# Gate and up products of layer 0's FFN by one level of Strassen's scheme (seven quarter-size products for eight)

## The reference

```
D_MODEL = 1024; D_FF = 2816
def channel_mixer(x, l, P):                     # layer 0
    h = rms_norm(x, P['norm_ffn'][l])
    a = silu(einsum('btd,df->btf', h, P['ffn_w_gate'][0])) * einsum('btd,df->btf', h, P['ffn_w_up'][0])
    return einsum('btf,fd->btd', a, P['ffn_w_down'][0])
```

## Time and profile before

| What | Value |
|---|---|
| three runs, median (lowest to highest) | 1901.38 us (1901.1 to 1902.55) |
| span of the profiled execution, first to last instruction | 1898.2 us |
| TensorE matmul busy | 1845.5 us (97%) |
| VectorE busy | 519.3 us (27%) |
| ScalarE busy | 365.9 us (19%) |
| gate and up products of layer 0, first to last start | 569.4 to 725.9 us |

### The profile page before, as it was taken

The page is one execution under the profiler, slowest core; times in us unless marked ns, Lnnn a source line. Parts: engine busy times, 40 slices in busy tenths (PEclk is TensorE's granted clock), DMA queues, the critical chain, the costliest instruction groups (busy, mean ns, idle before and its releaser), DMA issues.

```text
span 1898.2 us, 28175 instructions
## 1 busy us (share of the span) xinstructions
PE 1845.5 (97%) x11949; PEld 1285.5 (68%) x11949; DVE 519.3 (27%) x1150; ACT 365.9 (19%) x754; POOL 135.2 (7%) x226
## 2 busy tenths in 40 slices
PE   8999999999999999999999999999799999999998
PEld 5889878786678888878888878777533343433434
DVE  3454441527321000043635234363310000000000
ACT  2241334332010000014214333310110000100101
POOL 3000001304100000000100020220000000000000
PEclk9999999999999999999999999999899999999999
DMA  9833699999999978698429998999739999599992
GB/s 273 278 116 115 218 309 326 348 317 373 358 372 376 319 280 309 221 330 315 141 73 305 337 356 307 336 384 333 266 121 371 366 387 405 221 341 386 374 409 112
DMA packets 254690, 563.83 MB, mean 297 GB/s; under 512 B 11949, under 2 KB 149393, under 8 KB 254288
## 3 DMA queue, kind: packets, MB, share of 16 engines
q1 hardware_dynamic: 235232, 500.14, 74.3%
q0 software_dynamic: 18544, 58.58, 9.2%
q10 hardware_dynamic: 784, 3.25, 0.5%
HBM read 547.74 MB, written 196.63 MB: 392 GB/s over the span
## 4 chain that ended last, share of the span: by engine, by line
PE 94%; DMA 2%; DVE 2%; issue 1%; ACT 1%; POOL 0%; ACTq 0%; DVEq 0%; POOLq 0%
PE PS L867 33%; PE PS L1414 15%; PE PS L794 8%; PE PS L1440 8%; PE PS L1315 4%; PE PS L1275 4%; PE PS L787 3%; PE PS L1289 3%; PE PS L911 3%; PE PS L1376 2%; PE PS L904 2%; PE PS L1462 1%; PE PS L1211 1%; PE PS L802 1%; PE PS L1185 1%
## 5 line engine op out<-in xcount | busy, mean ns | idle before, releaser
L867 PE MATMUL PS<-h,ring 128*128 128x264 f32 x2816 | 655.2, 389 | 0.0
L867 PEld LDWEIGHTS PS<-h,ring 128*128 128x128 f32 x2816 | 528.5, 191 | 106.9 <-issue 21.3
L1579 ACT COPY z<-PS 128x264 f32<-128x264 f32 (+3 forms) x307 | 130.5, 444 | 854.2 <-PE PS L867 529.2
L1414 PE MATMUL PS<-ring,z 128*32 128x512 f32 (+1 forms) x1440 | 210.5, 522 | 1.2 <-ACT z L1579 1.2
L1414 PE MATMUL PS<-arena,z 128*32 128x512 f32 (+1 forms) x1056 | 190.1, 535 | 0.0
L1414 PEld LDWEIGHTS PS<-ring,z 128*32 128x32 f32 x1440 | 68.0, 110 | 125.7 <-issue 110.1
L794 PE MATMUL PS<-h,ring 128*128 128x264 f32 x512 | 115.3, 386 | 1.6 <-DVE h L1967 1.6
L794 PEld LDWEIGHTS PS<-h,ring 128*128 128x128 f32 x512 | 97.2, 190 | 18.6 <-issue 2.0
L1440 PE MATMUL PS<-arena,z 128*32 128x512 f32 x432 | 104.0, 593 | 0.0
L1414 PEld LDWEIGHTS PS<-arena,z 128*32 128x32 f32 x1056 | 55.0, 110 | 53.5 <-issue 53.4
L1275 PE MATMUL PS<-z,ring 128*128 128x264 f32 x384 | 87.3, 388 | 0.0
(11 more groups left out here) (319 smaller groups left out, 1805.5 us busy)
## 6 DMA issues: line engine op xcount, KB each, us to landing
out_win_s<-in_cache_win_kv SPq DMA_DIRECT2D x128, 1023.5 KB, 11.1
ring<-in_w_in SPq DMA_DIRECT2D x88, 1024.0 KB, 6.7
out_win_s<-in_cache_win_kv SPq DMA_DIRECT2D x32, 1022.0 KB, 14.1
ring<-in_moe_w_gate SPq DMA_DIRECT2D x28, 1024.0 KB, 9.7
arena<-in_moe_w_up SPq DMA_DIRECT2D x22, 1024.0 KB, 11.5
ring<-in_moe_w_up SPq DMA_DIRECT2D x22, 1024.0 KB, 8.7
ring<-in_moe_w_down SPq DMA_DIRECT2D x20, 1024.0 KB, 11.0
arena<-in_moe_w_down SPq DMA_DIRECT2D x18, 1024.0 KB, 10.4
```

Of the source, the lines that this page charges most:

```text
L867: last = mm(bank(l, "p", j)[:, 0:T], w[:, k, P * (j % 2):P * (j % 2) + P], h[:, k, :], start=(k == 0), stop=(k == KT - 1))
L1414: last = mm(m_bank("c", "gu", g, b, w, r)[BLK * j:BLK * j + BLK, 0:n], hs[:, k, P * r + BLK * j:P * r + BLK * j + BLK], v3(slot_ap(set_slo ...
L1579: return nc.scalar.copy(out, in_)
```

## The change

A chunk holds 256 columns and 1024 features, so it is cut into four quarters, [4 feature tiles of 128] by [128 columns]: a11 and a12 for the first column tile, a21 and a22 for the second (first index the column tile, second the half of the features). `h` is cut too, by features and by token columns, 132 each: h11, h12, h21, h22. The products of a chunk, which were 16 matmuls of 264 columns, become seven products of 4 matmuls of 132 columns, 28 in all. The form is the one with four sums on either side: for the weights s1 = a21 + a22, a21 <- a11 - a21 (in place, called s3), s2 = a22 - s3, s4 = a12 - s2; for `h` four sums once (`hd`). The seven results stand in four half-filled bank pairs ("xa", "ya", "xb", "yb"; some products add into the same half) and VectorE adds them up.

VectorE makes all weight sums (`weight_sums`, four operations of 128x512 for a chunk), those of the first three chunks between `wo` and `xnorm`, later ones three chunks ahead of their use; the four sums of `h` (`input_sums`); and the sums of the results (`first_sums`, `second_sums`). ScalarE takes silu in two parts. The slot of a chunk is released when "yb" of that chunk is full. The names of some semaphores that nothing used are dropped as well. The core of the diff:

```diff
-                for i in range(FF // P):
-                    plan((0, "fg", i), 2 * (i % 2))
-                    plan((0, "fu", i), 2 * (i % 2) + 1)
+                for q in range(CH_FFG):
+                    for name in ("xa", "ya", "xb", "yb"):
+                        plan((0, name, q), 2 * (q % 4) + (name[0] == "y"))
...
-                    place(CH_MIX + q, q % RING_F, (0, "fu" if q % 2 else "fg", 2 * (q // 2) + 1))
+                    place(CH_MIX + q, q % RING_F, (0, "yb", q))
...
+            def product(out, left, right, opens=False):
+                for k in range(4):
+                    last = mm(out, left[:, k, :], right[:, k, :], start=(opens and k == 0), stop=(k == 3), skip_group_check=True)
+                return last
+
+            def pair_first(q):
+                wait_chunk(pe, CH_MIX + q)
...
+                if q == 0:
+                    pe.wait_ge(sems["h_ready"], V("h_ready", 0, 11))
+                open_bank(pe, 0, "xa", q)
+                x_, y_ = bank(0, "xa", q), bank(0, "ya", q)
+                product(x_[:, 0:HT], a11, h11, True)
+                pe.wait_ge(fw_odd, q + 1)
+                pe.wait_ge(hd_ready, 1)
+                open_bank(pe, 0, "ya", q)
+                product(y_[:, 0:HT], s1, hd[0], True)
+                pe.wait_ge(hd_ready, 2)
+                product(y_[:, HT:T], s3, hd[2]).then_inc(full(0, "ya", q), 1)
+                pe.wait_ge(fw_even, 2 * q + 1)
+                pe.wait_ge(hd_ready, 3)
+                product(x_[:, HT:T], s2, hd[1]).then_inc(full(0, "xa", q), 1)
+
+            def pair_second(q):
...
+                open_bank(pe, 0, "xb", q)
+                product(x_[:, 0:HT], a12, h[:, 4:8, 0:HT]).then_inc(full(0, "xb", q), 1)
+                open_bank(pe, 0, "yb", q)
+                pe.wait_ge(hd_ready, 4)
+                product(y_[:, HT:T], a22, hd[3])
+                pe.wait_ge(fw_even, 2 * q + 2)
+                product(y_[:, 0:HT], s4, h[:, 4:8, HT:T]).then_inc(full(0, "yb", q), 1)
+
             def ffn0():
-                for i in range(FF // P):
...
+                pair_first(0)
+                for q in range(CH_FFG):
+                    if q + 1 < CH_FFG:
+                        pair_first(q + 1)
+                    pair_second(q)
...
+            def weight_sums(q):
+                wait_chunk(dve, CH_MIX + q)
+                a11, a12, a21, a22 = quarters(q)
+                if q >= 4:
+                    wait_full(dve, 0, "yb", q - 4)
+                s1, s2, s4 = sums(q)
+                tt(s1, a21, a22, ADD)
+                tt(a21, a11, a21, SUB).then_inc(fw_odd, 1)
+                dve.wait_ge(fw_odd, q + 1)
+                tt(s2, a22, a21, SUB).then_inc(fw_even, 1)
+                dve.wait_ge(fw_even, 2 * q + 1)
+                tt(s4, a12, s2, SUB).then_inc(fw_even, 1)
+
+            def input_sums():
...
+                dve.wait_ge(sems["h_ready"], V("h_ready", 0, 15))
+                tt(hd[0], h12, h11, SUB).then_inc(hd_ready, 1)
+                tt(hd[2], h22, h12, SUB).then_inc(hd_ready, 1)
+                dve.wait_ge(hd_ready, 1)
+                tt(hd[1], h22, hd[0], SUB).then_inc(hd_ready, 1)
+                dve.wait_ge(hd_ready, 3)
+                tt(hd[3], h21, hd[1], SUB).then_inc(hd_ready, 1)
+
+            def first_sums(q):
...
+                wait_full(dve, 0, "ya", q)
+                nc.vector.tensor_reduce(e_, y_[:, 0:T].rearrange("p (w t) -> p t w", w=2), AX.X, ADD).then_inc(free(0, "ya", q), 1)
+                wait_full(dve, 0, "xa", q)
+                nc.vector.tensor_reduce(v_, x_[:, 0:T].rearrange("p (w t) -> p t w", w=2), AX.X, ADD).then_inc(free(0, "xa", q), 1)
+                if q + 3 < CH_FFG:
+                    weight_sums(q + 3)
...
+                tt(out[:, 3 * HT:4 * HT], v_, e_, ADD)
+
+            def second_sums(q):
...
+                wait_full(dve, 0, "yb", q)
+                tt(v3(out[:, HT:3 * HT], 2), v3(y_[:, 0:T], 2), bc(fve[:, q % 2, 0, :], 1, [P, 2, HT]), ADD).then_inc(
+                    free(0, "yb", q), 1)
...
+                tt(fa2(i)[:, 0:HT], bank(0, "xb", q)[:, 0:HT], fs[i % 2][:, 0:HT], MUL).then_inc(free(0, "xb", q), 1)
+                wait_read(dve, 0, "yb", q)
+                tt(fa2(i)[:, HT:4 * HT], fup[:, HT:4 * HT], fs[i % 2][:, HT:4 * HT], MUL)
+                dve.drain().then_inc(fa_ready, 1)
...
+                if l == 0:
+                    for q in range(3):
+                        weight_sums(q)
                 settle()
                 xnorm(l, 1)
```

More of the change, by code:

```diff
@@ L635, in build, with fa2, quarters, sums @@
         fa = z[:, 8:8 + FF // P, :]
-        fs = z[:, 32:36, :]
-        ft = z[:, 36:40, :]
+        HT = T // 2
+        fs = [z[:, 32 + 2 * n:34 + 2 * n, :].rearrange("p a b -> p (a b)") for n in range(2)]
+        hd = [z[:, 40 + 2 * n:42 + 2 * n, :].rearrange("p a b -> p (a b)").rearrange("p (k t) -> p k t", k=4) for n in range(4)]
+        fw = [v3(arena[:, 2 * CW + 1536 * n:2 * CW + 1536 * n + 1536], 12) for n in range(3)]
+        fw.append(v3(z[:, 48:54, :].rearrange("p a b -> p (a b)")[:, 0:1536], 12))
+        fup = z[:, 54:56, :].rearrange("p a b -> p (a b)")
+        fve = z[:, 56:58, :].rearrange("p a b -> p (a b)").rearrange("p (n w t) -> p n w t", n=2, w=2)
+        def fa2(i):
+            return fa[:, 2 * i:2 * i + 2, :].rearrange("p a b -> p (a b)")
+        def quarters(q):
+            w = v3(chunk(CH_MIX + q), KT)
+            return w[:, 0:4, 0:P], w[:, 4:8, 0:P], w[:, 0:4, P:2 * P], w[:, 4:8, P:2 * P]
+        def sums(q):
+            return [fw[q % 4][:, 4 * n:4 * n + 4, :] for n in range(3)]
         zm = z[:, 0:Z_G, :].rearrange("p a b -> p (a b)")
@@ L1294, in wo @@
                 norm_part(l, 1, KT - 1)
-            def ffn0():
-                for i in range(FF // P):
-                    for w_, name in enumerate(("fg", "fu")):
-                        n = CH_MIX + 2 * (i // 2) + w_
-                        if i % 2 == 0:
-                            wait_chunk(pe, n)
-                        open_bank(pe, 0, name, i)
-                        w = v3(chunk(n), KT)
-                        dense((0, name, i), lambda k: w[:, k, P * (i % 2):P * (i % 2) + P], 0,
-                              1 if i == 0 and w_ == 0 else None)
+            def product(out, left, right, opens=False):
+                for k in range(4):
+                    last = mm(out, left[:, k, :], right[:, k, :], start=(opens and k == 0), stop=(k == 3), skip_group_check=True)
+                return last
@@ new lines, in pair_second @@
+            def pair_second(q):
+                _, a12, _, a22 = quarters(q)
+                s4 = sums(q)[2]
+                x_, y_ = bank(0, "xb", q), bank(0, "yb", q)
+                open_bank(pe, 0, "xb", q)
[5 more added lines that the diff above has]
+                product(y_[:, 0:HT], s4, h[:, 4:8, HT:T]).then_inc(full(0, "yb", q), 1)
@@ L1310, in ffn0 @@
                         k = 2 * q + w_
-                        wait_read(pe, 0, "fu", k)
+                        pe.wait_ge(fa_ready, k // 2 + 1)
                         for d in range(KT):
@@ L1835, in _ @@
                 if l == 0:
-                    for i in range(FF // P):
-                        hidden(0, i)
+                    for i in range(FF // P // 2):
+                        hidden(i)
                     logs_and_exponents()
@@ L2409, in wo @@
                     tt(x[:, d, :], x[:, d, :], bank(l, "wo", d)[:, 0:T], ADD).then_inc(free(l, "wo", d), 1)
-            def ffn0():
-                for i in range(FF // P):
-                    wait_read(dve, 0, "fg", i)
-                    wait_full(dve, 0, "fu", i)
-                    tt(fa[:, i, :], fs[:, i % 4, :], bank(0, "fu", i)[:, 0:T], MUL).then_inc(free(0, "fu", i), 1)
+            def weight_sums(q):
[10 more added lines that the diff above has]
+                tt(s4, a12, s2, SUB).then_inc(fw_even, 1)
@@ new lines, in input_sums @@
+            def input_sums():
+                h11, h12, h21, h22 = (h[:, 4 * k:4 * k + 4, HT * t:HT * t + HT] for k in range(2) for t in range(2))
+                dve.wait_ge(sems["h_ready"], V("h_ready", 0, 15))
[5 more added lines that the diff above has]
+                tt(hd[3], h21, hd[1], SUB).then_inc(hd_ready, 1)
@@ new lines, in first_sums @@
+            def first_sums(q):
+                out = fup if q % 2 else fs[q // 2 % 2]
+                x_, y_ = bank(0, "xa", q), bank(0, "ya", q)
+                v_, e_ = fve[:, q % 2, 0, :], fve[:, q % 2, 1, :]
+                wait_full(dve, 0, "ya", q)
[4 more added lines that the diff above has]
+                    weight_sums(q + 3)
+                wait_read(dve, 0, "ya", q)
+                wait_read(dve, 0, "xa", q)
+                tt(out[:, 3 * HT:4 * HT], v_, e_, ADD)
@@ L2416, in ffn0 @@
+            def ffn0():
+                input_sums()
+                first_sums(0)
+                for q in range(CH_FFG):
+                    if q + 1 < CH_FFG:
```

(2 more changed lines are left out.)

37 lines of the change are left out of this document (27 added, 10 removed).

## The result

Four runs of the changed kernel gave a median of 1889.64 us (1887.68 to 1891.69), four of the kernel before 1901.85 us (1901.1 to 1902.55): a ratio of 0.9934, interval 0.9921 to 0.9948. The profiled execution has a span of 1889.8 us and a time of 1891.69.

What follows compares the result with a forecast made beforehand. TensorE was taken to bound the kernel. Products -18.1, start +8.5, clock +2.2 and first weight loads +0.2 gave -7.2 us: span 1898.2 to 1891.0, median 1901.4 to 1894.2, with a range of about 1890 to 1901.

Steps and rivals of the forecast that it cites:

- What bounds the kernel: Whole kernel: TensorE, busy 97% of the span, holds the chain; only shortening its program or its waits helps.
- the stage's sum: Layer 0's gate and up stage: -18.1 + 8.5 + 2.2 + 0.2 = -7.2 us.
- Products: Gate and up matmuls: 1232 records of 132 columns at 0.1125 us, 138.6 us, 18.1 less than 156.7.
- the two bounds: Price of a 132-column record: 111.4 and 114.7 ns as bounds around 112.5, gain 15.4 to 19.5 us.
- VectorE in the steady state: VectorE's sums per chunk: mean 4.7 to 5.7 us, below TensorE's 6.3, so hidden and costing nothing.
- the slow rate of the 1022 ns row: VectorE operations at the rate of 1022 ns for 512 elements; as a rival, VectorE bounds, kernel at 1910; 8%.
- Start: Start of the stage: twelve weight sums ahead of `h` and a late second product, 7.0 + 1.5 = 8.5 us lost.
- Clock: TensorE after its idle time at the stage's start: granted clock 0.50 for a while, 2.2 us lost, bounds 0 and 3.6.
- first weight loads: TensorE's first weight loads after the waits: 0.2 us added.
- Weight loads: Rival in the narrow products: 190 ns loads no longer hide behind 110 ns of streaming, kernel at 1911 or 1990; 5%.
- The case in which a record costs 0.163 or 0.19: Narrow products: 0.163 us a record gives about 1956 us, 0.19 gives 1990; weight loads rival, 5%.
- Everything behind and ahead of the stage only shifts: Outside the stage: down products reached at 718.9 instead of 726.1 us, and everything behind shifts.

Runs made afterwards that it cites:

- narrow matmuls: The kernel before, each gate and up matmul of 264 columns split into two of 132, no sums: 1901.95 us, ratio 1.0002; FFN stage 194.40 us.
- More sums: The changed kernel with four more unused 128x512 VectorE additions per chunk from chunk 3 on: 1900.34 us, ratio 0.9989; FFN stage 191.43 us.
- clock kept: The changed kernel with dummy matmuls ahead of and behind its first product: 1893.02 us, ratio 0.9961; FFN stage 181.99 us.
- sums early: The changed kernel, chunk 0's weight sums moved into VectorE's wait inside `wo`, those of chunks 1 and 2 behind the sums of `h`: 1886.27 us, ratio 0.9915.
- Dead code: The kernel before with 280 matmuls and 180 VectorE additions in a branch never taken: 1900.42 us, ratio 0.9994; attention stage 96.23 us.
- before again: The kernel before, unchanged, measured again as a control: 1903.61 us, ratio 1.0006; attention stage 98.55 us.
- semaphores only: The kernel before with only the change's semaphore bookkeeping, unused ones dropped and six added: 1902.26 us, ratio 0.9999; attention stage 98.42 us.

## Why the prediction was right, and where it was wrong

**What bounds the kernel, and the stage's sum: right, term by term.** The stage gained 7.55 us where the sum said 7.2.
- *Products*, forecast 0.1125 us a record: starts stand 112 or 113 ns apart, and 0.1125 in the mean, here and in narrow matmuls. The value between the two bounds (slope from wider matmuls, floor from narrower ones) held.
- *VectorE in the steady state*, forecast 4.7 us of a chunk's 6.3: it waits 2.1 us, so it took 4.2, a tenth less. A reduction over the pair took 0.43 and the 396-wide addition 0.56, as forecast; the slow rate of the 1022 ns row did not apply to any of them. More sums shows that the limit was where it was put.
- *Start*, forecast 8.5: twelve sums took 8.05, as forecast. `wo` ended 0.5 us earlier in this profile, so TensorE began 6.6 + 0.5 = 7.1 us late; its second product, due 0.9 us after the first, started 2.36 after it, 1.5 lost. Sum 8.6.
- *Clock*, forecast 2.2: 1.2 GHz from 568.6 to 582.2. The first product hides its slowness in the wait for the second; from 578.36 to 582.2 half of 3.84 us is lost, 1.9, and clock kept gave 1.90 back. The sum is then -18.1 + 8.6 + 1.9 = -7.6; of the 0.2 us for first weight loads nothing shows.
- *Weight loads*: a load is still recorded 190 ns long, and 135.80 of 135.80 us are busy with loads at 112 ns a record. They overlap each other. The case in which a record costs 0.163 or 0.19 did not come. The Trainium skill, TensorE: Matmul & The Clock Gate, Back-to-back issue gap, puts a stream of loads and matmuls at 81 ns where the isolated gap is 56; as a ratio for these fp32 records, the trace speaks against it. The same page of the Trainium skill, section LDWEIGHTS, gives 107 ns for a load of 128 columns, and the 111.4 ns of the 128-column groups stand near that.

Of these terms, the start is shown by sums early, the clock by clock kept, VectorE's limit by more sums and the price of a record by narrow matmuls. That the sum comes within 0.4 us is better than its terms: the clock's term moves by 0.6 us between two executions of the same program.

**What failed is the step from the stage to the whole.** The prediction put it so: "The profiled execution would go from 1898.2 to 1891.0, and the median of runs, 3.2 us above the span, from 1901.4 to 1894.2." Two things are wrong in it.
- *Everything behind and ahead of the stage only shifts.* The prediction put the change outside the stage at nothing. The runs leave about 3 us there: 1902.4, the median of the 87 runs of before made beside the experiments, less 7.6 for the stage is 1894.8, against 1891.6 measured. One place is known: the attention stage, which ends some 130 us ahead of the first gate product, took 2.2 us less. Dead code reproduces this to the hundredth (96.23) with nothing else changed; the semaphores alone do not. But the profiles do not carry it whole to the end, and dead code and narrow matmuls, which have it, came out at ratios of 0.9994 and 1.0002, no difference that can be told. The first `wo` product begins at 534.4 to 534.8 in the three profiles of before, before again and semaphores only, and at 534.14 and 532.66 in the two of after, 0.3 to 2.1 earlier. Behind the first down product stand 1172.1 to 1174.8 us against 1171.8 and 1171.5, 0.3 to some 3.3 less; of that, layer 1's attention stage took 97.0 to 97.8 us against 96.2 and 95.9. So the 3 us lie on both sides of the stage, and only the attention stage of layer 0 has an experiment behind it.
- *The base.* The span that I subtracted from was short for its kernel: those 87 runs of the same program came to 1897.3 to 1909.8, median 1900.5. And the 3.2 us compared the span of one run with the median of others. The forecast of 1894.2 still took a median as its base, 1901.4, which was 1.0 low; this moved the number little. But I drew the low end of the range, 1890.0, from bounds of the terms alone, with nothing for runs that differ by 2 to 5 us. The first four runs of after gave 1889.64; nine give 1891.6, inside the range. That the first four fell on the far side of 1890.0 was chance; that they lay so near it was not.

**Left open:** what it is in a longer TensorE program that lets a transfer land sooner. Its address in memory, that of the data behind it, or the fetching of instructions would all fit; none was tried apart. Nor is it settled why the half clock lasts 3.4 us in one program and 6.8 in another when the tables land alike, or what shortened layer 1.

## What to carry to other kernels

A narrower matmul can be priced from one wider and one narrower shape in the same trace; take both ends, and the value between. With a form that trades products for sums, look at the first chunk first: here the sums in front of the first product took 8.6 of 18.1 us, and placing them in an engine's existing waits gave back 6, and 8 once the clock was kept and the reductions that free a bank went first. Then leave room for what the program's size does to stages that it doesn't touch: compare a stage with itself and with where it starts, run the kernel before with code that never executes, and let the range take in what runs of one program differ by, before some 2 us are credited to an idea.

## What the hardware showed that I had not expected

- 280 matmuls that are never executed brought the landing of a 384 KB transfer from 9.3 to 9.7 down to 8.3 us, with 180 VectorE additions beside them to 7.8; those additions alone, 10.1. The whole kernel's time changed by 0.15% or less (ratios 0.9985, 0.9994 and 1.0005).
- The starts of fp32 matmul records of 132 columns stand 112.5 ns apart for 145 us on end while each one's weight load is recorded 190 ns long; nothing of the load shows.
- The granted clock fell to 0.50 behind an idle time of 8.75 us and also behind one of 2.8 us (sums early), and came back after 13.6 and 6.8 us. With dummy matmuls in the gaps, and 0.74 us still idle ahead of the first product (clock kept), it didn't fall.
